# Sample attention woven into the prompt's first four tiles, and later transposes on two pairs of banks in the normed projections of a streaming encoder layer

## The reference

```python
z, xbc, dt_raw, q, k, v = jnp.split(rms_norm(x, g_pre_mix) @ w_in, IN_SPLITS, axis=-1)
...                                             # state-space scan gives y_ssd (512 columns)
k_all = jnp.concatenate([k_past, rope(k)], axis=1)   # prompt: no past; sample: 256 past keys each
s = jnp.einsum('bqhcd,bkhcd->bhcqk', q, k_all) / math.sqrt(64)      # 4 heads, c = 2 halves
p = jax.nn.softmax(jnp.where(visible, s, -jnp.inf), axis=-1)
att = p[:, :, 0] - lam * p[:, :, 1]
o = jnp.einsum('bhqk,bkhe->bqhe', att, v_all)
o = o * lax.rsqrt(jnp.mean(o * o, -1, keepdims=True) + 1e-5) * subln_w * (1.0 - lam_init)
mix = jnp.concatenate([y_ssd, y_att], axis=-1) @ w_out
h = x + rms_norm(mix, g_post_mix)
qx = rms_norm(h, g_pre_x) @ wq_x
...                                             # cross attention, 4 heads of 256, 256 memory tokens
h = h + rms_norm(ox @ wo_x, g_post_x)
hn = rms_norm(h, g_pre_ffn)
h = h + rms_norm((silu(hn @ w_gate) * (hn @ w_up)) @ w_down, g_post_ffn)
```

## Time and profile before

| | |
|---|---|
| median of 3 runs | 2066.97 us (2064.14 to 2067.23) |
| profiled execution | 2071.4 us, span 2069.2 us |
| mean granted TensorE clock | 0.958 of full |
| TensorE products busy | 1911.7 us (92% of the span) |
| TensorE weight loads busy | 1785.2 us (86%) |
| VectorE busy | 822.7 us (40%) |
| ScalarE busy | 521.7 us (25%) |
| GpSimd busy | 512.6 us (25%) |

### The profile page before, as it was taken

The page is one execution under the profiler, slowest core; times in us unless marked ns, Lnnn a source line. Parts: engine busy times, 40 slices in busy tenths (PEclk is TensorE's granted clock), DMA queues, the critical chain, the costliest instruction groups (busy, mean ns, idle before and its releaser), DMA issues.

```text
span 2069.2 us, 29594 instructions
## 1 busy us (share of the span) xinstructions
PE 1911.7 (92%) x12155; PEld 1785.2 (86%) x12155; DVE 822.7 (40%) x1642; ACT 521.7 (25%) x1265; POOL 512.6 (25%) x299
## 2 busy tenths in 40 slices
PE   7999999877788778989989989999999999999997
PEld 7999899866566668989978989999999999999995
DVE  5354116685767723361353271213213312322327
ACT  5200112275366533242343251000010010010002
POOL 3444342131000002212200312222232331421423
PEclk9999999897669989999999999999999999999998
DMA  5333331111400250131063421101111110110132
GB/s 207 113 121 106 99 128 41 58 28 36 161 1 1 80 211 31 42 133 52 29 236 123 163 112 41 41 31 51 41 41 41 41 51 30 51 51 20 61 114 100
DMA packets 59461, 161.24 MB, mean 78 GB/s; under 512 B 4192, under 2 KB 18016, under 8 KB 59104
## 3 DMA queue, kind: packets, MB, share of 16 engines
q1 hardware_dynamic: 36768, 115.04, 15.8%
q10 hardware_dynamic: 22592, 44.81, 6.2%
HBM read 131.67 MB, written 28.16 MB: 77 GB/s over the span
## 4 chain that ended last, share of the span: by engine, by line
PE 79%; DVE 10%; ACT 5%; issue 3%; DMA 1%; POOL 0%; ACTq 0%; SPq 0%; DVEq 0%; POOLq 0%
PE bank L224 24%; PE bank L227 23%; PE bank L228 23%; DVE at_sm L1749 2%; PE bank L958 1%; PE bank L262 1%; DVE ACC L1985 1%; DVE H L337 1%; DVE E L1683 1%; PE bank L865 1%; ACT E L1318 1%; DMA V<-out_v 1%; PE bank L755 1%; DVE ATT L1769 1%; PE bank L727 1%
## 5 line engine op out<-in xcount | busy, mean ns | idle before, releaser
L563 POOL CAST w_hi<-w_raw 128x1024 fp32r<-128x1024 f32 x130 | 140.4, 1080 | 1422.0 <-PE bank L224 1399.1
L224 PE MATMUL bank<-OH,w_hi 128*128 128x384 f32 x1056 | 355.1, 336 | 0.0
L228 PE MATMUL bank<-OH,w_lo 128*128 128x384 f32 x1056 | 354.8, 336 | 0.0
L227 PE MATMUL bank<-OL,w_hi 128*128 128x384 f32 x1056 | 354.8, 336 | 0.0
L565 POOL TENSOR_TENSOR w_lo<-w_raw,w_hi 128x1024 fp32r<-128x1024 f32 x130 | 325.9, 2507 | 10.4
L228 PE MATMUL bank<-w_hi,NL 128*128 128x256 f32 x864 | 244.7, 283 | 0.0
L1965 DVE TENSOR_TENSOR hr<-sg,bank 128x384 f32<-128x384 f32 x66 | 36.6, 554 | 438.1 <-PE bank L228 437.1
L227 PEld LDWEIGHTS bank<-OL,w_hi 128*128 128x128 f32 x1056 | 198.5, 188 | 0.4
L224 PEld LDWEIGHTS bank<-OH,w_hi 128*128 128x128 f32 x1056 | 198.5, 188 | 0.4
L228 PEld LDWEIGHTS bank<-OH,w_lo 128*128 128x128 f32 x1056 | 198.5, 188 | 0.0
L1979 DVE TENSOR_TENSOR ACC<-ACC,bank 128x512 f32<-128x512 f32 x180 | 122.8, 685 | 109.3 <-PE bank L228 109.3
(11 more groups left out here) (329 smaller groups left out, 3760.4 us busy)
## 6 DMA issues: line engine op xcount, KB each, us to landing
w_raw<-in_wall SPq DMA_DIRECT2D x130, 512.0 KB, 3.3
scratch_h<-H ACTq DMA_DIRECT2D x6, 1536.0 KB, 5.3
MIX<-in_cmk SPq DMA_DIRECT2D x8, 1024.0 KB, 5.3
cV<-in_cmv SPq DMA_DIRECT2D x8, 1024.0 KB, 5.1
H<-in_x SPq DMA_DIRECT2D x1, 4608.0 KB, 14.7
H<-scratch_h SPq DMA_DIRECT2D x1, 4608.0 KB, 16.2
Hback<-scratch_h ACTq DMA_DIRECT2D x1, 4608.0 KB, 14.0
out_y<-Hback SPq DMA_DIRECT2D x9, 512.0 KB, 2.6
```

Of the source, the lines that this page charges most:

```text
L224: m = mm(out, ah, bh, start=(i == 0), stop=False)
L227: mm(out, ah, bl, start=False, stop=False)
L228: m = mm(out, al, bh, start=False, stop=(i == n - 1))
L563: pool.tensor_copy(whi[s][:], raw[s % 2][:]).then_inc(w_hi, 1)
```

## The change

First, the serial sample attention is taken out. Sample b = 0 to 7 is worked in the prompt's units u = 2b and 2b + 1, in banks and buffer parts that the tiles 0 to 3 leave free (B[1], B[3], B[5]; the right ends of the E and ATT buffers). Its scores are four products over 32 query columns, one per head, into 32 rows each; values likewise; a product with a 0/1 matrix `Sum` joins the halves. Cached keys and values go through two slots each, in the place of weight slots 2 and 3, loaded after the xBC projection. GpSimd splits items 42 and 43 after the last sample. At u = 15 scores(16) wait until sample 7 is done. The samples' output is transposed at u = 17, normed on ScalarE, scaled on VectorE and transposed back at u = 18. High and low parts are made tile by tile, and o_trans(7) comes after the projection's second unit.

Second, in both normed projections pre_trans, pre_hi and pre_lo of tile t come two units later (n = 31 + t, the last four behind the next product's first units), the tiles 1, 3 and 5 use B[4], B[5]. Third, in the cross attention x_values(s) moves behind the next unit's scores from s = 5 to 7 (`LATE`).

```diff
 # TensorE, attention
+            def s_scores(b):
+                pe.wait_ge(ld_kb[b % 2], 16 * (b // 2 + 1))
+                if b:
+                    pe.wait_ge(b_exp, b)
+                else:
+                    pe.wait_ge(b_q, 1)
+                for h in range(H):
+                    mm(B[1][32 * h:32 * h + 32, 0:PAST], g("Qs")[:, h, b, :], kring(b)[:, h, :], start=True, stop=True)
+                for h in range(H):
+                    m = mm(B[1][32 * h:32 * h + 32, PAST:PAST + DS], g("Qs")[:, h, b, :], g("KTs")[:, h, DS * b:DS * b + DS],
+                           start=True, stop=True)
+                m.then_inc(b_S, 1)
...
+            def s_values(b):
+                pe.wait_ge(b_Te, b + 1)
...
+                for k in range(3):
+                    for h in range(H):
+                        v = vring(b)[:, k, tok(h)] if k < 2 else g("V")[:, NT - 1, tok(h)]
+                        m = mm(B[3][32 * h:32 * h + 32, 0:P], PTb[:, P * k + 32 * h:P * k + 32 * h + 32], v, start=(k == 0),
+                               stop=(k == 2))
+                m.then_inc(b_pv, 1)
...
             scores(0)
+            s_scores(0)
             for u in range(U):
-                if u + 1 < U:
+                b = u // 2
+                if u + 1 < U and u != 2 * DB - 1:
                     scores(u + 1)
                 probs_turn(u)
+                if u < 2 * DB:
+                    if u % 2:
+                        s_values(b)
+                        if b + 1 < DB:
+                            s_scores(b + 1)
+                    else:
+                        if b:
+                            s_sum(b - 1)
+                        s_trans(b)
                 if u:
                     values(u - 1)
+                if u == 2 * DB - 1:
+                    s_sum(DB - 1)
+                    pe.wait_ge(b_o, DB)
+                    scores(u + 1)
 # ScalarE, attention
             exps(0)
+            s_exp(0)
             for u in range(U):
+                if u == 2 * DB - 1:
+                    copy_pt(u)
+                    s_out(DB - 1)
+                    s_out_t(DB - 1)
+                    exps(u + 1)
+                    continue
                 if u + 1 < U:
                     exps(u + 1)
                 copy_pt(u)
+                if u < 2 * DB:
+                    if u % 2:
+                        s_out(b)
+                        s_exp(b + 1)
+                    else:
+                        if b:
+                            s_out_t(b - 1)
+                        s_copy(b)
                 if u % H == 1 and u > H:
                     o_norm(u // H - 1)
...
+                if u == 17:
+                    act.wait_ge(b_nb, DB + 1)
+                    o_squares(g("QTs")[:].rearrange("p h q -> p (h q)"), 24, 28, 52).then_inc(b_exp, 1)
 # VectorE, attention
+            link(nc.vector.memset(g("Qs")[:], 0.0))
...
             maxes(0)
+            s_max(0)
             for u in range(U):
                 probs(u)
+                if u < 2 * DB and u % 2 == 0:
+                    s_probs(b)
...
+                if u == 18:
+                    dve.wait_ge(b_exp, DB + 1)
+                    TT(onS, onS, bc(asm[:, 52:56].unsqueeze(2), [P, H, DH]), ALU.mult).then_inc(b_p, 1)
                 if u + 1 < U:
                     maxes(u + 1)
+                if u < 2 * DB - 1 and u % 2:
+                    s_max(b + 1)
 # the start of the first projection: ScalarE, VectorE, TensorE
+            y_high(0)
+            y_high(1)
+            y_high(2)
             o_evac(NT - 3)
+            o_norm(NT - 2)
+            for t in (3, 4, 5, 6, 8):
+                y_high(t)
+            o_evac(NT - 2)
+            y_high(7)
...
+            y_low(0)
+            y_low(1)
             o_copy(NT - 2)
+            for t in (2, 3, 4):
+                y_low(t)
+            o_scale(NT - 2)
+            for t in (5, 6, 8, 7):
+                y_low(t)
...
                 join_unit(pe, 0, I_WO, n, YH, NL)
-                if n >= 27 + 2:
-                    pre_trans(pe, Z_J1 + n - 29, g("MIX")[:, n - 29, :])
+                if n == 1:
+                    o_trans(NT - 2)
+                if n >= 27 + 4:
+                    pre_trans(pe, Z_J1 + n - 31, g("MIX")[:, n - 31, :])
 # normed projections
+        def turn_low(z):
+            return z >= Z_J1 and (z - Z_J1) % NT in (1, 3, 5)
+        def turn_bank(z, j):
+            return B[4 + j] if turn_low(z) else B[6 + j]
...
-                if t >= 2:
-                    pre_lo(dve, z0 + t - 2, hi[:, :, tok(t - 2)], lo[:, :, tok(t - 2)])
+                if t >= 4:
+                    pre_lo(dve, z0 + t - 4, hi[:, :, tok(t - 4)], lo[:, :, tok(t - 4)])
 # cross attention, TensorE
+                if s >= LATE + 1:
+                    x_values(s - 1)
                 x_trans(s)
                 if len(fill) > 1:
                     lin_unit(pe, I_WQ, fill[1], YH, NL)
-                x_values(s)
+                if s < LATE:
+                    x_values(s)
 # SP's queue
-            sp.wait_ge(a_exp, 2 * H * (NT - 1))
-            for b in range(6):
...
+            sp.wait_ge(xb_mm, 3 * KT)
+            for b in range(DB):
+                if b >= 2:
+                    sp.wait_ge(b_S, b - 1)
+                sp.dma_start(kring(b), kc[b]).then_inc(ld_kb[b % 2], 16)
...
-            sp.wait_ge(b_pv, 4)
+            sp.wait_ge(b_S, DB)
             sp.dma_start(g("H")[:], x_in.rearrange("(t p) c -> p t c", p=P)).then_inc(ld["res"], 16)
```

More of the change, by code:

```diff
@@ L105, in build @@
         T = {}
+        for half in ("hi", "lo"):
+            T.update(overlay([(f"w_{half}{i}", [P, WI], F32R) for i in range(4)],
+                             [(f"under_{half}", [P, 2, WI], F32)] +
+                             [(f"kring{i}", [P, H, PAST], F32) if half == "hi" else (f"vring{i}", [P, 2, 512], F32)
+                              for i in range(2)]))
+        whi, wlo = [T[f"w_hi{i}"] for i in range(4)], [T[f"w_lo{i}"] for i in range(4)]
+        stat = sb("stat", [P, S_END])
+        cst = sb("cst", [P, C_END])
+        vec = sb("vec", [P, V_END])
+        ones = sb("ones", [P, P])
+        eps6 = sb("eps6", [P, 1])
+        eps5 = sb("eps5", [P, 1])
+        nlam = sb("nlam", [P, 1])
+        lams = sb("lams", [P, 2])
+        coef = sb("coef", [P, 1])
+        cred = sb("cred", [P, 5])
         T.update(overlay([("H", [P, NT, D], F32)],
@@ L442, in build @@
                                       "onorm", "otrans", "oout"))
-        ld_kb = [sem(f"ld_kc{i}") for i in range(DB // 2)]
+        ld_kb = [sem(f"ld_cache_{x}{i}") for x in ("keys", "values") for i in range(2)]
         b_q, b_S, b_nb, b_exp, b_p, b_T, b_Te, b_pv, b_o = (
@@ new lines, in s_trans @@
+            def s_trans(b):
+                pe.wait_ge(b_p, b + 1)
+                if b:
+                    pe.wait_ge(b_Te, b)
+                for k in range(2):
+                    nc.tensor.transpose(B[5][:, tok(k)], Es[:, tok(k)], ident)
+                nc.tensor.transpose(B[5][:, tok(2)], Pn[b % 2], ident).then_inc(b_T, 1)
+            def s_values(b):
+                pe.wait_ge(b_Te, b + 1)
+                pe.wait_ge(ld_kb[2 + b % 2], 16 * (b // 2 + 1))
+                if b:
+                    pe.wait_ge(b_o, b)
+                else:
+                    pe.wait_ge(ld_v, 16)
+                for k in range(3):
[4 more added lines that the diff above has]
+                m.then_inc(b_pv, 1)
@@ L1537, in _ @@
             for n in range(6 * NG):
-                gate(n)
-                hid_high(n)
+                for half in (gate, hid_high):
+                    if n < 2:
+                        t = 5 + 2 * n + (half is hid_high)
+                        pre_hi(act, Z_J2 + t, OH[:, :, tok(t)])
+                    half(n)
             act.wait_ge(f_up, 12 * NG)
@@ L1857, in _ @@
-            o_copy(NT - 1)
-            for c in range(CH):
-                dve.wait_ge(yh_s, c + 1)
-                TT(NL[:, :, cs(c)], g("YT")[:, :, cs(c)], YH[:, :, cs(c)].bitcast(F32), ALU.subtract).then_inc(yl_s, 1)
-                if c == 0:
-                    o_scale(NT - 1)
+            for t in (2, 3, 4):
[3 more added lines that the diff above has]
+                y_low(t)
+            dve.wait_ge(yl_s, NT)
+            dve.wait_ge(ld["gB0"], 32)
@@ L1865, in _ @@
             dve.wait_ge(ld["res"], 16)
-            dve.wait_ge(ld["gB0"], 32)
             dve.wait_ge(ld["gB1"], 32)
-            dve.wait_ge(yl_s, CH)
             join_dve(dve, 0, 0, g("MIX"), H_, YH, NL, Z_J1)
+            for t in range(5, NT):
+                pre_lo(dve, Z_J1 + t, YH[:, :, tok(t)], NL[:, :, tok(t)])
             xm = g("xm")
@@ L1988, in _ @@
                 for n in range(6 * gi, 6 * gi + 6):
+                    for t in (5 + 2 * n, 6 + 2 * n) if n < 2 else ():
+                        pre_lo(dve, Z_J2 + t, OH[:, :, tok(t)], OL[:, :, tok(t)])
                     hid_raw(n)
```

340 lines of the change are left out of this document (151 added, 189 removed).

## The result

The changed kernel takes 2031.2 us (median of 4 runs, 2029.91 to 2031.86), the kernel before on the same chip 2065.6 us (4 runs, 2056.39 to 2067.23): ratio 0.9842, interval 0.982 to 0.9863, a gain of 34 us by the medians and 32.6 by the ratio. Forecast were 2019 us and a gain of 48, with a range of 2005 to 2036. The profiled execution took 2031.5 us, span 2029.7; spans shrank by 39.5 us, since the profiled execution of before lay above its median.

A forecast was written before the change was run, and what follows sets the result against it. It took VectorE and ScalarE's ping-pong to bound the attention loop, with TensorE hidden, and bank waits the projections. 62.1 - 5.0 - 28 + 14 + 5 = 48 us off 2071.4 gives 2023, less 4.4: 2019 us, range 2005 to 2036.

The forecast's parts named there:

- Change 1: Serial sample attention before the first projection goes: 62.1 us removed, less a 5.0 us stall after two projection units.
- (a): Start of the attention loop: clearing, copies and small tables on VectorE before the first maximum cost 2.6 us.
- (b): Even units of the loop: VectorE's scaling of the sample weights costs 1.0 us, eight times, 8.0 us.
- (c): Odd units: the sample maxima wait for TensorE's sample products, 10.0 us more, less 3.2 for output copies slipping into the wait.
- the coupling: In the loop, in-order waits between ScalarE's copies and TensorE add 2 us.
- The clock: TensorE in tiles 0 to 3 was taken at full clock, granted over 0.9; loop cost 28 us, bound 41 at half.
- (d): Unit 15: the next unit's scores wait until sample 7 is finished; 5.1 us more, 0.9 of it counted in (c).
- (e): Unit 17: ScalarE norms the sample output behind tile 3's norm, lengthening ATT(17) to ATT(19) by 4.5 us; TensorE work hidden.
- Change 3: Later transposes on two bank pairs in the normed projections: gain 7 us (3 to 10) each, 14 in all.
- Change 4: Last cross-attention steps: values a step later gain 5 us (2 to 7), with some 2.7 us more wait for memory keys.
- The offset: The runs' median, 2067.0 us, lies 4.4 below the profiled execution, so 2023 became 2019 us.
- the loop at 1.2 GHz: Rival: TensorE stays at the slow clock in the loop, 13 us more, 2032 us; chance 0.17.

The follow-up runs named there:

- e2: The kernel before with only the later transposes on two pairs of banks in both normed projections: 2054.1 us, ratio 0.9955.
- e3: The kernel before with only the cross attention's values one step later in the last steps: 2057.1 us, ratio 0.996.
- e5: The changed kernel with unit 16's scores and exponentials split by halves, the first half issued earlier: 2024.9 us, ratio 0.9811.
- e8: The kernel with spread norm and split unit 16, the sample weights' scaling moved from VectorE into ScalarE's copy of the sample output: 2015.5 us, ratio 0.9767.
- e10: The changed kernel with 16 of the 24 value products of each sample left out, so its output is not the reference's: 2023.7 us, ratio 0.9814.
- e11: The changed kernel with 44 unread filler transposes ahead of the first sample scores and four more in each of 11 units: 2023.8 us, ratio 0.9817.
- e9: e8 with the last sample output's sum and most of unit 16's scores moved ahead of the values of unit 14: 2012.7 us, ratio 0.975.
- e1: The changed kernel with the sample output's norm spread over units 17 to 22, behind the next units' maxima: 2018.6 us, ratio 0.9775.
- e7: The changed kernel with 44 unread filler transposes in TensorE's wait ahead of the first sample scores: 2031.5 us, ratio 0.984.

## Why the prediction came out as it did

The result lies in the range, 12 us above the forecast. By its own steps, the prediction's value first:

- **Change 1**: 62.1 removed, 61.7 measured (72.6 less 10.9); the stall 5.0 against 4.2. H was not late: the first gain starts at 771.9 us without a wait for it. "About 34 us earlier": 26.7 earlier (757.28), by the loop.
- **(a)**, 2.6: the first ATT began 0.7 us later, but it varies by more than this term from trace to trace; not settled. Among traces with the quick pace ahead of the loop it began at 544.6 and 545.9 us without the weave (e2, e3) and at 546.7 and 550.4 with it (e5, changed).
- **(b), (c) and the coupling**, 8.0 + 9.1 - 3.2 + 2 = 15.9 for these steps (0.9 of the 10.0 belong to the eighth pair, under (d)): the 15 steps grew by 14.7. The eight even to odd ones grew by 8.0, which is (b), the seven odd to even ones by 6.7. The distances in tile 0 were named as 3.8 and 4.4 and are 3.57 and 4.51; e8 and e10 show the two causes. VectorE's waits at s_max are 7.6 us in seven, 1.7 at most.
- **The clock**: named as over 0.9 in tiles 0 to 3; it was 0.73 (first window after). That was wrong, and the time of these steps was near the forecast nonetheless, which is luck. e11 suggests how: at a higher clock the same steps take 73.0 us, a growth of 10.3. The full-clock terms were then 5 to 6 us too high, mostly in the odd to even steps (3.1 us of growth there in e11), and the slow clock filled that.
- **(d)**, 5.1 with its share in (c): 6.8, with the values at 1.90 us where 0.9 was put, in a step with a granted clock of 0.64. e9 confirms the chain.
- **(e)**, 4.5: **12.1, the mis-sized term**. The step that failed is the sentence "the TensorE work of these units hides beneath". Much more than 4.5 us behind the sample's norm was among the prediction's own signs of being wrong. It counted ScalarE's second norm alone. It left out that the sample output's copy waits 4.71 us for transposes that stand behind the turn of unit 17 and the values of unit 16, with the maxima of unit 18 behind the copy; ScalarE stood idle 6.9 us, and tile 3's norm, with the sample's behind it, began later. The step from ATT 17 to 18 grew by 5.4 us (5.40 to 10.81) by that wait, the one from 18 to 19 by 6.7 (6.49 to 13.20) by the second norm and VectorE's scaling behind it. e1 shows it: same norm, 10.9 us less.
- **Change 3**, 14: the first joint gave 4.9 (the query's copy is 27.4 us earlier, the projection's start 26.7, and the stall of 4.2 lies between; both traces have the slow pace there), the second 6.8 (what is left of the span's 39.5). Together 11.7; e2's ratio gives 9 within 3. The waits of 5 us were named.
- **Change 4**, 5: 4.2 to the first sample product and 1.1 behind it; the new wait 3.4 against 2.7.
- **The offset**: the forecast took off 4.4 us because the profiled execution of before lay above its median. That of after lies at its median. This, with the 7 us of the loop (35.0 with its start, 711.34 to 746.36, against 28) and 2 of change 3, makes up the missing 14 us of gain; the rest is what medians of before differ by.

Of the rivals, the loop at 1.2 GHz named 2032, which is the number measured; but of its 13 us some 6 are seen (4.4 in the 15 steps, up to 1.7 in (d)), and the largest part of what was missing, 7.6 us, is (e). That its number was hit is chance. Changes 3 and 4 did give. Turns between forms cost no 3 us each: the odd to even step grew by 1.7 us in all. The Trainium skill (TensorE: Matmul & The Clock Gate, Part 1) says that activity releases the clock; e11 agrees (0.87 for 0.74 from 560 to 600 us), but the weave alone brought the tiles 0 to 3 from 0.62 to 0.73 and no further. The Trainium skill (TensorEngine Tiling (Array Packing), Key Properties) also says that changing the tiling mode drains TensorE; that would cost at the same turns, and no run here separates it from the products.

## What to carry to other kernels

Work woven into a loop costs more at its tail than in its regular steps: list for each one-off step what it waits for and what stands behind it in the same engine's order, and put it behind the next round's work on the path. Here moving such steps won 12.6 us, over a third of what the whole change did. And check a forecast of the clock by itself: here the clock was missed (over 0.9 forecast, 0.73 granted) and the steps' time was hit, because the full-clock terms were too high by about what the slow clock cost.

## What the runs showed of the hardware

44 useless transposes ahead of a loop brought TensorE's granted clock from 0.50 to 1.00, and it stayed there for 5 us of the loop (e7); in another trace with the same 44 (e11) the loop's first two steps ran at 0.50. Four more in the gaps of each of 11 units went with a granted clock of 0.87 instead of 0.74 (560 to 600 us) and with shorter steps, although they added 44 transposes.

At the same granted clock of 1.00 and with TensorE always busy, the same 24 products took 2.72 us in ten traces and 2.83 us in four. This and the loop's own spread (76.6 to 79.3 us for the 15 steps, 544.6 to 555.2 us for the first ATT) mean that one trace's difference of 3 us in such a stretch needs a second trace.
